# Moving small steps between the engines' in-order queues in the pipelined RWKV layer of a two-block model

## The reference, cut to what matters

```python
w_log = -softplus(-(w0 + tanh(xw @ w1) @ w2)) - 0.5
decay = exp(-exp(w_log))
a = sigmoid(a0 + (xa @ a1) @ a2)
kk = normalised(k * k_k)                    # per head
k = k * (1.0 + (a - 1.0) * k_a)
# per token: state = state*decay + (state @ -kk)(kk*a)^T + v k^T;  out = state @ r
o = group_norm(out) * gn_w + gn_b
o = (o + sum(r * k * r_k) * v) * silu(g)
y = o @ w_o
```

## Time and profile before

| what | value |
|---|---|
| median of 3 runs | 2589.24 us (2589.03 to 2593.2) |
| the profiled execution's own time | 2589.24 us |
| its span in the profile | 2587.4 us |
| PE busy over the span | 2468.1 us (95%) |
| DVE / ACT / POOL busy | 58% / 48% / 7% |
| stretch of the eight-group pipeline | some 2229 to 2470 us of the span |

### The profile page before, as it was taken

How to read it: one execution, slowest core, us unless ns; L and a number is a source line. 1 busy time by engine, 2 the same in 40 slices (tenths; PEclk the granted TensorE clock), 3 DMA queues, 4 the chain that set the end, 5 groups by cost and what they waited for, 6 DMA issues and landing times.

```text
span 2587.4 us, 38999 instructions
## 1 busy us (share of the span) xinstructions
PE 2468.1 (95%) x15976; PEld 2051.8 (79%) x15976; DVE 1494.9 (58%) x1964; ACT 1253.3 (48%) x1656; POOL 179.1 (7%) x208
## 2 busy tenths in 40 slices
PE   8999999999999999999999999999799999989897
PEld 6886888878788878787887888878688888778785
DVE  5457555575566566665444544445657555678666
ACT  5446444574555555554444444434435445455443
POOL 2002000000000000000000100000000001134320
PEclk9999999999999999999999999999899999899998
DMA  7756666555555555556555565535446677323352
GB/s 245 240 176 145 203 203 203 198 192 191 185 185 174 176 195 179 174 178 237 191 193 195 188 195 167 171 102 194 171 163 220 219 231 249 103 54 84 100 196 98
DMA packets 242409, 463.41 MB, mean 179 GB/s; under 512 B 9952, under 2 KB 39849, under 8 KB 240480
## 3 DMA queue, kind: packets, MB, share of 16 engines
q1 hardware_dynamic: 223488, 422.08, 49.2%
q0 software_dynamic: 18464, 39.22, 5.5%
q10 hardware_dynamic: 320, 0.13, 0.0%
HBM read 446.66 MB, written 14.74 MB: 178 GB/s over the span
## 4 chain that ended last, share of the span: by engine, by line
PE 46%; DVE 5%; ACT 2%; issue 1%; ACTq 0%; DVEq 0%
PE bank L324 13%; PE bank L325 13%; PE bank L326 13%; PE bank L2076 2%; PE bank L1917 1%; DVE d_products L2046 1%; PE bank L2146 1%; PE bank L2477 1%; PE bank L2173 1%; PE bank L1559 0%; ACT w_high L255 0%; DVE d_steps L2095 0%; DVE w_low L261 0%; PE bank L442 0%; PE bank L1901 0%
## 5 line engine op out<-in xcount | busy, mean ns | idle before, releaser
L261 DVE TENSOR_TENSOR w_low<-raw,w_high 128x1024 fp32r<-128x1024 f32 x768 | 929.1, 1221 | 836.8 <-ACT w_high L255 835.6
L255 ACT ACTIVATE w_high<-raw 128x1024 fp32r<-128x1024 f32 x768 | 804.9, 1057 | 956.4 <-PE bank L326 935.7
L324 PE MATMUL bank<-w_high,b_h_high 128*128 128x512 f32 x704 | 278.2, 395 | 9.0 <-DVE w_low L261 7.5
L326 PE MATMUL bank<-w_high,b_h_low 128*128 128x512 f32 x704 | 275.3, 391 | 0.0
L325 PE MATMUL bank<-w_low,b_h_high 128*128 128x512 f32 x704 | 275.0, 391 | 0.0
L324 PE MATMUL bank<-w_high,a_h_high 128*128 128x512 f32 (+1 forms) x640 | 247.6, 387 | 4.0 <-DVE w_low L261 2.3
L325 PE MATMUL bank<-w_low,a_h_high 128*128 128x512 f32 (+1 forms) x640 | 246.3, 385 | 0.0
L326 PE MATMUL bank<-w_high,a_h_low 128*128 128x512 f32 (+1 forms) x640 | 246.2, 385 | 0.0
L324 PE MATMUL bank<-w_high,d_high 128*128 128x512 f32 x512 | 203.1, 397 | 10.6 <-DVE d_low L2608 10.6
L324 PE MATMUL bank<-w_high,c_x_high 128*128 128x512 f32 x512 | 203.3, 397 | 0.6 <-DVE c_x_low L465 0.6
L325 PE MATMUL bank<-w_low,d_high 128*128 128x512 f32 x512 | 201.4, 393 | 0.0
(11 more groups left out here) (366 smaller groups left out, 3633.2 us busy)
## 6 DMA issues: line engine op xcount, KB each, us to landing
raw<-in_w_up SPq DMA_DIRECT2D x88, 1024.0 KB, 5.1
raw<-in_w_in SPq DMA_DIRECT2D x76, 1024.0 KB, 5.1
raw<-in_ev_w_in SPq DMA_DIRECT2D x48, 1024.0 KB, 5.1
raw<-in_w_down SPq DMA_DIRECT2D x44, 1024.0 KB, 5.0
raw<-in_w_out SPq DMA_DIRECT2D x16, 1024.0 KB, 5.0
raw<-in_ev_w_out SPq DMA_DIRECT2D x16, 1024.0 KB, 5.0
raw<-in_od_w_r SPq DMA_DIRECT2D x16, 1024.0 KB, 5.0
raw<-in_od_w_k SPq DMA_DIRECT2D x16, 1024.0 KB, 5.0
```

The source lines that it names most:

```text
L255: act.activation(wh[n % 4][:, :, 0:width], raw_half, ACT.Copy).then_inc(sem("w_high_made"), 1)
L261: vec.tensor_tensor(wl[n % 4][:, :, 0:width], raw_half, wh[n % 4][:, :, 0:width].bitcast(F32), ALU.subtract).then_inc(sem("w_low_made"), 1)
L324: pe.matmul(b, xh, wh[n][:, k % 2, 0:width], start=(c == 0 and k == 0), stop=False)
L326: mm = pe.matmul(b, xl, wh[n][:, k % 2, 0:width], start=False, stop=(c == j.chunks - 1 and k == 3))
```

## The change

Five edits, all in the last layer:

1. PE's prep part 1 (lora) is taken out of half 10 (and, for group 1, out of the place ahead of the pipeline) and put into half 1 behind stage 1Y. The step that it waits for becomes the last of the score steps.
2. DVE's `u` is moved from part 4 into part 3.
3. DVE's part 4, now `cs_before` alone, is moved from half 4 to half 3, ahead of the state step "s".
4. POOL's prep part 5 doesn't wait for DVE's step "a" (AQ) any more.
5. POOL's post part 4 doesn't wait for the step "0X1" of the group after next any more.

```diff
--- before.py
+++ after.py
@@ -1889,7 +1889,7 @@
         if part == 1:
             loaded(pe, n)
             if n >= 1:
-                await_step(pe, "score_vec", "01", n - 1)
+                await_step(pe, "score_vec", "11", n - 1)
             for i in range(2):
                 for t in range(2):
                     mm = pe.matmul(PS[6 + i][:, GW * t:GW * t + GW], TH[:, i, 128 * t:128 * t + 128], W2[n % 2][:, i, :],
@@ -1970,7 +1970,6 @@
                 await_step(gp, "state_pe", "s", n - 2)
             inc(gp.tensor_tensor(KH[par][:, :, :], tn[:, :, :], te[:, :, :], ALU.mult))
         if part == 5:
-            await_step(gp, "prep_vec", "a", n)
             if n >= 1:
                 await_step(gp, "prep_vec", "bonus_sum", n - 1)
             inc(gp.tensor_tensor(tb[:, :, :], r[:, :, :], tn[:, :, :], ALU.mult))
@@ -2003,9 +2002,9 @@
             await_step(vec, "prep_vec", "a1", n)
             inc(vec.scalar_tensor_tensor(out=tn[:, :, :], in0=tn[:, :, :], scalar=1.0, in1=k[:, :, :], op0=ALU.add,
                                          op1=ALU.mult))
-        if part == 4:
             inc(vec.scalar_tensor_tensor(out=ta[:, :, :], in0=ta[:, :, :], scalar=-1.0, in1=tk[:, :, :],
                                          op0=ALU.mult, op1=ALU.mult))
+        if part == 4:
             await_step(vec, "prep_act", "growth", n)
             inc(vec.tensor_tensor(tq[:, :, :], PS[6][:, :].rearrange("p (t n) -> p t n", t=2), tw[:, :, :],
                                   ALU.subtract))
@@ -2286,9 +2285,9 @@
     STATE_AT = {2: ["w", "xq"], 3: ["s"], 4: ["p1"], 5: ["p2", "o0"], 6: ["ru"]}
     POST_AT = {6: 1, 7: 2, 8: 3, 9: 4}
     SCORE_AT = {8: 0, 9: 1}
-    PE_AHEAD, PE_BEHIND = {3: [2]}, {6: [6], 7: [7]}
+    PE_AHEAD, PE_BEHIND = {3: [2]}, {1: [1], 6: [6], 7: [7]}
     ACT_AHEAD, ACT_BEHIND = {1: [1], 2: [2]}, {3: [3, 4], 4: [5], 6: [6], 7: [7]}
-    VEC_AHEAD, VEC_BEHIND = {3: [3]}, {1: [1], 2: [2], 4: [4, 5], 10: [8]}
+    VEC_AHEAD, VEC_BEHIND = {3: [3, 4]}, {1: [1], 2: [2], 4: [5], 10: [8]}
     POOL_AHEAD, POOL_BEHIND = {}, {4: [4], 5: [5]}
 
     def pipeline(eng, level, state, prep, post, score, first, last, ahead, behind):
@@ -2314,8 +2313,6 @@
                 if n + 1 < GROUPS and half in SCORE_AT:
                     score(eng, n + 1, SCORE_AT[half])
                     first(eng, n + 1, SCORE_AT[half])
-                if prep is prep_pe and (half == 10 and n + 2 < GROUPS):
-                    prep(eng, n + 2, 1)
                 if n < GROUPS and half == R0_AT:
                     state(eng, n, "r0")
                 if n == GROUPS:
@@ -2389,8 +2386,6 @@
             inc(gp.tensor_tensor(by_head(P2), by_head(RKVG[n % 3][2]), wide(DSM[:, n % 3, 16:24]), ALU.mult))
         if part == 4:
             await_step(gp, "post_vec", "norm", n)
-            if n + 2 < GROUPS:
-                await_step(gp, "first_vec", "0X1", n + 2)
             inc(gp.tensor_tensor(OO[:, :, :], OO[:, :, :], row(n, GNW), ALU.mult))
             await_step(gp, "post_pool", "gain", n)
             inc(gp.tensor_tensor(OO[:, :, :], OO[:, :, :], row(n, GNB), ALU.add))
@@ -2498,7 +2493,6 @@
         def last(pe, half):
             for n in EARLY.get(half, ()):
                 o_turn(pe, n)
-        prep_pe(pe, 1, 1)
         pipeline(pe, level_pe, state_pe, prep_pe, idle, score_pe, idle, last, PE_AHEAD, PE_BEHIND)
         await_step(pe, "state_act", "o0", GROUPS - 1)
         run_pe(pe, plan["odd_out"], turned_ready(pe, TD_o), None, lambda c: o_turn(pe, 7) if c == 2 else None)
```

## The result

The changed kernel takes 2621.98 us (median of 4 runs, 2621.8 to 2625.66), beside 2590.18 us of the kernel before (4 runs). The ratio is 1.0125, with a 95% interval of 1.0107 to 1.0142: it is 28 to 37 us slower. The forecast was 21.1 us slower. The direction was right, and so were the costs of edit 5 and of edits 2 to 4; the cost of edit 1 and what is given back were not. The sum was a third too small, and the time lies at the upper end of the range. The profiled execution of the changed kernel took 2616.85 us (span 2615.0), less than all four timed ones, so the profiles differ by 27.6 us where the medians differ by 31.8.

The account below looks back on a forecast made before the run. A chain passing between PE, DVE and ACT was taken to bound the kernel, no engine being full. The terms 9.9 + 8.0 + 7.2 - 0.5 - 3.5 gave 21.1 us over 2589.24: 2610.3 us, range 2598 to 2622.

Parts of the forecast that it names:

- edit 5: POOL's earlier post products take turns with DVE's level 0 masked copies; 0X1 1.33 us late in six iterations, 8.0 us.
- edits 2 to 4: Between `k_new` and 3Y's copy, POOL's products meet DVE's `u`, NEG_B, AQ; 1.2 us in six iterations, 7.2 us.
- the cost of edit 1: Lora behind 1Y loses its cover and PE starts 1T 1.65 us later in six iterations, 9.9 us.
- what is given back: PE's issue waits shrink as group loads start earlier and PE has new waits; 3.5 us taken, between 0 and 10.3.
- What bounds: A chain passing between engines sets the time: PE gapless from 1T to 2T, DVE ahead of 1Y; no engine full.
- Rival (a): The level 0 masked copies pass POOL unhindered, so 8.0 us less: 13.1 us slower, 2602.3 us; chance 0.20.
- the two orders: At `u`'s meeting with POOL: POOL first makes 3T 1.95 us late, `u` first 0.6; 1.2 taken.
- changes no sum by itself: Moving 1.6 us of DVE work ahead of state step "s" leaves the stretch from `k_new` to 3Y's copy equally long.
- Rival (b): PE's issue waits stay whole, nothing given back: 24.6 us slower, 2613.8 us; chance 0.12.
- Rival (c): Unkind order throughout: 11.7 us for the DVE and POOL prep moves, 12 for the masked copies; 2618.8 us; chance 0.12.
- 32 to 34: Sign expected in the profile after: iterations of 32 to 34 us instead of 28.5 to 30.

Follow-up runs that it names:

- warm_more: The changed kernel plus a longer unused filler (six lora calls) at lora's old place in half 10; 2609.02 us, ratio 1.0055.
- warm_lora: The kernel before with only lora moved behind 1Y, and the product issued once more, unused, at its old place; 2597.32 us, ratio 1.0027.
- lora_alone: The kernel before with only lora moved behind 1Y; 2617.47 us, ratio 1.0088.
- post_alone: The kernel before with only POOL's post part 4 no longer waiting for 0X1; 2600.30 us, ratio 1.0036.
- steps_alone: The kernel before with only `u` and `cs_before` moved earlier and POOL's part 5 not waiting for AQ; 2598.16 us, ratio 1.0021.
- pool_alone: The kernel before with only POOL's prep part 5 no longer waiting for AQ; 2597.78 us, ratio 1.0025.
- u_early: The kernel before with only `u` and `cs_before` moved ahead of the state steps; 2594.96 us, ratio 1.0015.
- no_post: The changed kernel with POOL's post part 4 waiting for 0X1 again; 2613.12 us, ratio 1.0069.

## Why the prediction was right or wrong, point by point

**What bounds.** Right: the time goes along the chain, and PE from 1T to 2T and DVE ahead of 1Y were where it grew.

**Edit 1.** The step that failed is "1T, which started at 2324.28, starts there: 1.65 us later", that is, lora's cost as 1.93 us of PE behind 1Y (its own times give 1.67). The order was right: in the trace after, 1T starts directly behind lora. The size was wrong, because 1.93 us is lora's time at the full clock. Taken from its old place lora leaves a wait ahead of 1Y, and I counted that wait as empty time that costs nothing. It costs the clock of what follows, until about 2371 in the iteration shown: 3.85 us up to 1T instead of 1.65, and 1.81 more up to `k_new` (0.4 to 1.8 in the five iterations), where I had passed on the shift and added nothing. At the full clock the term holds: 1T is 1.63 us late in warm_more, and an iteration of warm_lora 1.60 longer. That the clock is the difference is shown by the changed kernel against warm_more, and by lora_alone against warm_lora. I never asked what the clock would be without lora in the wait. The trace of before had a sign of it, a mean of 0.61 from 2236 to 2251 us in iteration 0, which has longer waits, and one against it, the 1.00 behind waits of 0.69 and 1.45 us shown above; so it could have been a rival, with a price, but not a certainty. After the result, the Trainium skill ("TensorE: Matmul & The Clock Gate", "A second HAM failure mode: psum-queue depth-cycling") is worth reading beside this: it tells of a kernel whose TensorE idles so often between groups of matmuls that the clock moves between its two levels. The trace agrees: 1.35 and 2.06 us of waits, and 0.50 behind them.

**Edit 5.** Right in mechanism and size: 1.27 us per iteration, forecast 1.33, the copies 1.11 and 1.06, forecast 1.12 and 1.11. Rival (a) falls, and with it the only doubt about the term. The Trainium skill ("SBUF — State Buffer", "Who interferes with whom") says that a VectorE instruction with two SBUF inputs contends with a GpSimd instruction that reads SBUF; the trace agrees for this masked copy, 1.11 us instead of 0.45. So these two engines do not meet only at semaphores, against what the section on the cores says. Two masked copies with their data in PSUM keep their 0.77 us beside POOL in the changed kernel too (from 2355.92, POOL's product from 2356.08). The 9.4 us of post_alone hold some clock besides, which the forecast had not.

**Edits 2 to 4.** 1.41 us per iteration, forecast 1.2, between the two orders: `u` won the first meeting, but AQ lost its turn as well as NEG_B. steps_alone is 5.4 us slower by its ratio, forecast 7.2 - 0.5 less what is given back. That the wait of POOL for AQ is what kept these meetings away is shown by pool_alone (3Y's copy 1.38 us late). That moving `u` and `cs_before` "changes no sum by itself" was wrong by a little (u_early, 0.38 us per iteration).

**What is given back.** Forecast 3.5, measured 12.2 - 4.0 = 8.2 us over the same stretch of time and 10.0 - 4.0 = 6.0 over the same five iterations. The cause was left open and is half shown now: the waits come with the group loads. The Trainium skill ("Runtime: NRT & Kernel Launch", "Instruction fetch mechanics") calls instruction fetch mostly hidden. The trace has 12.2 us of issue waits beside the loads and 0.5 without them; that they are waits for fetching no view shows. Rival (b) falls. That fewer of them remained in the changed kernel because PE had more waits to hide them in is argued, not shown.

**The sum.** For a kernel whose clock holds, the three terms were right: 1.65 + 1.33 + 1.2 = 4.18 us per iteration, and warm_more has 4.29. What the sum lacks is the clock, 17.25 us over five iterations in the profiles; the medians give 13.0, and the profile of warm_more loses 8.2 ahead of these iterations. Its sign was there in the iterations, 35.4 to 36.5 us long and not 32 to 34. The other way goes what is given back, 2.5 to 4.7 us more than forecast, so two errors of opposite sign hid each other in part. With 8.2 in its place the forecast's terms give 24.6 - 8.2 = 16.4 us, and the median of warm_more is 16.5 above before (2609.02 against 2592.48); by its ratio it is 14.3 (10 to 18), so that the two agree to a tenth is luck. Rival (c) has the right size for the wrong reason: no term was at its unkind end. That the time still lies inside the range is luck too, as the range was made without the clock.

## What to carry to other kernels

A piece of work that fills PE's wait has two values: its own time, and the clock of what follows. Ask of each matmul that is moved out of a wait what PE does there instead, and read the granted clock in windows of a few microseconds, since a mean over the whole kernel all but hides it (0.979 in the changed kernel, 0.986 before). Whether an operation of POOL is free depends on which DVE operations stand beside it: with one that has two inputs in SBUF it takes turns, and each lasts longer. Waits for "issue" on an engine that runs a long unrolled list may come from the DMAs beside them.

## What the runs showed of the hardware that was not expected

- Doing the same product twice, once unused, made the kernel 20 us faster (2617.47 to 2597.32).
- The clock of PE fell to 0.50 behind waits of 1.25 and 1.45 us with 0.68 us of work between them in one iteration of lora_alone, and behind 0.69 and 1.45 in three more; behind the same 0.69 and 1.45 it held in another. One of its six iterations had lora at 1.99, the others between 3.29 and 3.78. The kernels in which the clock falls sometimes have the widest runs: 2609 to 2624 (lora_alone) and 2604 to 2624 us (no_post), against 2606 to 2611 for warm_more.
- With 11.26 MB of DMA traffic over 181 us, 62 GB/s in the mean and most of it group loads, PE had 12.2 us of issue waits; at 22 GB/s, most of it at the end of the stretch, 0.5 us were left.
- A masked copy with mask and data both in SBUF lasts 1.06 to 1.12 us beside POOL's products instead of 0.45.
